# Gate and up weights of an expert in rows of 16 KB and one transfer, in place of two arrays with rows of 8 KB

## The chip, the cores and the metric

One NeuronCore of a Trainium2 chip runs the whole program. The metric is the device time of one execution in microseconds (us), the median of several. The engines are TensorE (PE), VectorE (DVE), ScalarE (ACT), GpSimd (POOL) and SyncE (SP), which issues most transfers; 16 DMA engines move the data of all queues.

## What is computed

One layer of a decoder trunk for 1024 prompt tokens and 64 sample tokens, in float32: a projection, a convolution branch and a windowed attention branch, their merge, and a mixture of 32 experts with the top 2 of one group. The change touches the experts only:

```python
xb = xn[tok_buf].reshape(n_blocks, MOE_BLOCK, D_MODEL)       # MOE_BLOCK = 128, D_MODEL = 1024
def expert_block(args):
    xblk, e = args
    hid = jax.nn.silu(xblk @ w_gate[e]) * (xblk @ w_up[e])    # D_EXPERT = 256
    return hid @ w_down[e]
yb = lax.map(expert_block, (xb, blk_expert)).reshape(rows, D_MODEL)
return jnp.zeros_like(xn).at[tok_buf].add(yb * w_buf[:, None])
```

There are 1088 tokens and 2 experts for each, 2176 pairs, spread over at least 32 blocks of 128 slots.

## The kernel before

The phases run one behind the other. Norm, attention, sample, convolution and merge take the time up to 1163 us and have no part in the change. The last one, `ffn_phase`, first goes through 9 tiles of 128 tokens (output projection, norm, routing), then through the expert blocks.

**Data.** Matrix products have the precision of float32 by splitting each operand into a high and a low half in float16 and doing three products (`mm3`, lines 69 to 71). So each block's weights are loaded as float32 and then cut: ACT writes the high half, DVE the low half (float32 minus high). The gate and up weights of an expert are 8 chunks of 128 rows by 512 columns. The host lays them out by partition: 8 x 512 float32 numbers, 16 KB, for each of the 128 partitions. `layout` puts chunks 0 to 3 in `w_gu0` and chunks 4 to 7 in `w_gu1`, each with 8 KB a partition. `w_dn` has 8 KB a partition.

**Buffers.** There are four float32 buffers for `w_gu` and four for `w_dn` (`gu32`, `d32`; two of each in own tiles `e_gu`, `e_d`, one each inside `xnT` and `big`), and two of the cut halves (`gu`, `d`), one for even and one for odd blocks. Block b uses buffer b mod 2 for the first two, then (b - 2) mod 4.

**Loads (SP).** `load_expert` (lines 1569 to 1576) issues loads 0 to 7 at fixed places, `load_any` (lines 1612 to 1619) the rest in a loop of 6 rounds of four, blocks 8 to 31. Before it overwrites a buffer, SP waits until DVE has finished with the half in question: `gu_low[0]` and `gu_low[1]` count DVE's subtractions of half 0 and half 1, `d_low` those of `w_dn`. SP issues in order: half 0, half 1, `w_dn`.

**Gathers and scatters (POOL).** Tokens of a block are gathered from `hn_dram` by an indirect DMA (line 1656), and the weighted results added into `y_all` by another (line 1667), 4 KB a row. A block's pairs fill its slots from partition 0 upwards; slots without a pair are out of bounds and move nothing. Both have two buffers, so a gather or scatter has to be over two blocks later. Ahead of the loop the pairs themselves are scattered to DRAM (line 1643) and loaded back by SP.

**A block in the loop.** ACT's `body(b)`: gate, cut of half 0 of block b + 2 (line 1734), result of block b - 1 (line 1761, waits for the scatter of b - 3), rows of block b + 2 (1744), hidden (1754), cut of half 1 of block b + 2 (1734), cut of `w_dn` of block b + 1 (1740). DVE's `body(b)`: gate (1968, 1971), low half of half 0 (1951), rows (1962), hidden (1975), low half of half 1 (1951), low half of `w_dn` (1957). PE: gate-up of block b, down of b - 1, turn of b + 2 (2089), turn of the hidden rows (2107).

Of the kernel before, what the change touches and what calls it, by code (L numbers as in the profile page):

```python
# [20 lines left out]
ds = bass.ds  # L21
# [3 lines left out]
KC = D // P  # L25
# [1387 lines left out]
def ffn_phase(nc, sem, g, A):  # L1413


    with ExitStack() as c:
# [103 lines left out]
                                    "scat", "ctl"))  # L1520
        pairs_ld, late_ld, xg_zero, all_out = sem("e_pairs_ld"), sem("e_late_ld"), sem("e_xg_zero"), sem("e_all_out")
        gather_go, scatter_go = sem("e_gather_go"), sem("e_scatter_go")
        gu_ld = tuple((sem("e_gu_ld0" + n), sem("e_gu_ld1" + n)) for n in "abcd")
        d_ld = tuple(sem("e_d_ld" + n) for n in "abcd")
        xg_ld = (sem("e_xg_ld0"), sem("e_xg_ld1"))
        y_st = (sem("e_y_st0"), sem("e_y_st1"))
# [29 lines left out]
        @block.sync  # L1556
        def _(sp):
            def load_x(t):
                if t > 2:
                    sp.wait_ge(h_st, 16 * (t - 2))  # L1560
                    sp.wait_ge(hn_done, t - 2)
                sp.dma_start(x_in[:, t % 3], A["x_all"][t * P:(t + 1) * P, :]).then_inc(x_ld[t % 3], 16)

            def store_h(t):
                sp.wait_ge(h_done, t + 1)
                sp.dma_start(A["y_all"][t * P:(t + 1) * P, :], x_in[:, t % 3]).then_inc(h_st, 16)

            def load_expert(b, f, used):
                for half in range(2):
                    if used:  # L1570
                        sp.wait_ge(gu_low[half], used)
                    sp.dma_start(gu32[f][:, halves[half]], A[("w_gu0", "w_gu1")[half]][b].rearrange("p (k n) -> p k n", k=HK)
                                 ).then_inc(gu_ld[f][half], 16)
                if used:
                    sp.wait_ge(d_low, used)
                sp.dma_start(d32[f], A["w_dn"][b].rearrange("p (k n) -> p k n", k=2)).then_inc(d_ld[f], 16)

            load_x(0)
            sp.dma_start(r32, A["w_rt"]).then_inc(r_ld, 16)
            sp.dma_start(gain[:], rows_on_partitions(A["norm_ffn_g"], P, D)).then_inc(gain_ld, 16)  # L1580
            load_x(1)
            sp.dma_start(rb[:], rows_on_partitions(A["b_rt"], P, RP)).then_inc(rb_ld, 16)
            load_x(2)
            sp.dma_start(iota[:], A["c_iota"]).then_inc(iota_ld, 16)
            sp.dma_start(upper[:], A["c_upper"]).then_inc(upper_ld, 16)
            sp.dma_start(A["pair_dram"].rearrange("(p n) a -> p (n a)", p=P), A["c_unused"]).then_inc(unused_st, 16)
            load_expert(0, 0, 0)
            load_expert(1, 1, 0)
            for t in range(TT):
                store_h(t)  # L1590
                if t + 3 < TT:
                    load_x(t + 3)
                if t == 4:
                    load_expert(2, 0, 1)
                if t == 6:
                    load_expert(3, 1, 2)
            sp.wait_ge(mm, TT)
            load_expert(4, 2, 0)
            load_expert(5, 3, 0)
            by_column = A["pair_dram"].rearrange("(p n) a -> n p a", p=P)  # L1600
            sp.dma_start(pairs[:, NE:].rearrange("p b a -> p (b a)"), A["c_unused"][:, 0:4 * NOV]).then_inc(late_ld, 16)
            sp.wait_ge(scat, 16 * 2 * TT)
            sp.dma_start(pairs[:, 0:NE], A["pair_dram"].rearrange("(p n) a -> p n a", p=P)[:, 0:NE]).then_inc(pairs_ld, 16)
            load_expert(6, 0, 3)
            load_expert(7, 1, 4)
            few = rounds(sp)
            sp.wait_ge(late_ld, 16)
            for i in range(NOV):
                col = sp.value_load(ctl[0:1, NBLK + i:NBLK + i + 1], min_val=0, max_val=NCOL - 1)  # L1609
                sp.dma_start(pairs[:, NE + 2 * i + 1], by_column[ds(col, 1)].rearrange("n p a -> (n p) a")).then_inc(late_ld, 16)  # L1610

            def load_any(b, f):
                e = sp.value_load(ctl[0:1, ds(b, 1)], min_val=0, max_val=NE - 1)
                for half in range(2):
                    sp.wait_ge(gu_low[half], b - 3)
                    sp.dma_start(gu32[f][:, halves[half]].rearrange("p k n -> p (k n)"),
                                 A[("w_gu0", "w_gu1")[half]][ds(e, 1)].rearrange("a p n -> (a p) n")).then_inc(gu_ld[f][half], 16)
                sp.wait_ge(d_low, b - 3)
                sp.dma_start(d32[f].rearrange("p k n -> p (k n)"),
                             A["w_dn"][ds(e, 1)].rearrange("a p n -> (a p) n")).then_inc(d_ld[f], 16)  # L1620

            with sp.Fori(0, few) as v:
                for q in range(4):
                    load_any(4 * v + 8 + q, (q + 2) % 4)
# [86 lines left out]
        def _(act):  # L1711
# [18 lines left out]

            def cut(load, p, half):
                f, need = load
                act.wait_ge(gu_ld[f][half], need)
                act.activation(gu_h[:, p, halves[half]], gu32[f][:, halves[half]], ACT.Copy,  # L1734
                               scale=S_W).then_inc(gu_high[half], 1)

# [501 lines left out]
def layout(x_prompt, x_sample, state_conv, cache_k, cache_v, norm_attn_g, w_in, q_norm_g, k_norm_g, rel_bias,  # L2238
           attn_sinks, w_dw, b_dw, conv_ln_g, conv_ln_b, w_conv_out, b_conv_out, w_attn_out, w_out, norm_ffn_g,
           w_grp, b_grp, w_router, b_router, w_gate, w_up, w_down):  # L2240

    f = np.float32
    x_all = np.zeros((TP, D), f)
    x_all[0:SEQ] = x_prompt.reshape(SEQ, D)
    x_all[SEQ:T] = x_sample.reshape(TS, D)

    def chunks(w):

        return w.reshape(KC, P, -1, P).transpose(2, 1, 0, 3).reshape(-1, P, KC * P)

    def by_channel(v):
        return v.reshape(KC, P).T


    gated = np.stack([chunks(w_in[:, COL_GB:COL_GB + D]), chunks(w_attn_out)], 1).reshape(2 * KC, P, KC * P)
    bag = np.stack([chunks(w_in[:, c:c + D]) for c in (COL_B, COL_A, COL_GA)] + [gated[0:KC]], 1)
    def in_turn(w):

        return w.reshape(NG, EPG, P, -1).transpose(1, 0, 2, 3).reshape(NE, P, -1)

    gu = in_turn(np.concatenate([w_gate, w_up], 2).reshape(NE, KC, P, 2 * DE).transpose(0, 2, 1, 3))
    dn = in_turn(w_down.reshape(NE, 2, P, D).transpose(0, 2, 1, 3))

    dist = 2 * P - 1 - np.arange(RW)
    n = np.maximum(dist, 0)
    large = NB // 2 + (np.log(np.maximum(n, 1).astype(f) / f(NB // 2)) / f(np.log(128 / (NB // 2)))
                       * f(NB - NB // 2)).astype(np.int32)
    bucket = np.where(n < NB // 2, n, np.minimum(large, NB - 1))
    inside = (dist >= 0) & (dist < WIN)
    c_bucket = ((bucket[None, :] == np.arange(NB)[:, None]) & inside[None, :]).astype(f)  # L2270
    c_mask = np.broadcast_to(np.where(inside, f(0), f(NEG)), (NH, RW))
    return {k: np.ascontiguousarray(v) for k, v in {
        "x_all": x_all, "norm_attn_g": norm_attn_g, "w_in": w_in, "gq2": np.concatenate([q_norm_g] * 2)[:, None],
        "k_norm_g": k_norm_g, "rel_bias": rel_bias, "attn_sinks": attn_sinks,
        "cache_k": cache_k.reshape(NSEQ, WIN, KVW), "cache_v": cache_v.reshape(NSEQ, WIN, KVW),
        "ckT": cache_k.transpose(3, 2, 0, 1).reshape(HD, NKV * NSEQ, WIN),
        "cvT": cache_v.transpose(1, 0, 2, 3).reshape(WIN, NSEQ, KVW),
        "stateT": state_conv.transpose(2, 0, 1), "tapsT": w_dw.T.reshape(KC, P, TAPS).transpose(1, 0, 2),
        "conv_vecs": np.stack([by_channel(b_dw), by_channel(conv_ln_g), by_channel(conv_ln_b)], 1),
        "b_conv_outT": by_channel(b_conv_out),  # L2280
        "w_feat": np.concatenate([bag.reshape(-1, P, KC * P), gated[KC:], chunks(w_conv_out)]),
        "w_out": w_out, "norm_ffn_g": norm_ffn_g,
        "w_rt": np.concatenate([w_grp, np.zeros((D, 8 - NG), f), w_router], 1).reshape(KC, P, RP).transpose(1, 0, 2),
        "b_rt": np.concatenate([b_grp, np.full(8 - NG, NEG, f), b_router]), "w_gu0": gu[:, :, 0:gu.shape[2] // 2], "w_gu1": gu[:, :, gu.shape[2] // 2:], "w_dn": dn,
        "c_ident": np.eye(P, dtype=f), "c_bucket": c_bucket, "c_mask": c_mask,
        "c_iota": np.broadcast_to(np.arange(NE, dtype=f), (P, NE)),
        "c_upper": np.triu(np.ones((P, P), f), 1), "c_unused": unused_slots()}.items()}
# [23 lines left out]
```

## Time and profile before

| | us |
|---|---|
| median of 3 runs (1677.76 to 1679.7) | 1678.14 |
| the profiled execution | 1678.61 |
| its span, first to last instruction | 1677.0 |
| expert blocks, from the first gather to the end | 376.0 |

| engine | busy us | share of the span |
|---|---|---|
| PE | 1335.1 | 80% |
| DVE | 1147.2 | 68% |
| ACT | 637.7 | 38% |
| POOL | 249.1 | 15% |

The hardware queue q1 carries SP's transfers, 32416 packets and 156.99 MB; the software queue q0 carries POOL's, 16144 packets and 36.84 MB. A busy share of DMA is the mean over the 16 engines: a share of 0.68 can be all engines busy two thirds of the time, or two thirds of them busy all the time. Shares over an average of the whole span hide stages; the expert blocks have the last 376 us.

### The profile page before, as it was taken

To read this page: it belongs to the slowest core of one execution; us is meant where nothing else is said; L and a number is where in the kernel's file an instruction comes from. 1 tells how busy PE (TensorE), PEld (TensorE's weight loads), DVE (VectorE), ACT (ScalarE), POOL (GpSimd) and SP (SyncE) were. 2 spreads that over 40 slices of the span, in tenths; PEclk is the share of its full clock that TensorE was granted. 3 is DMA by queue.
4 is the path that set the end of the run, shared out by engine and by line. 5 is a ranking of instruction groups with operands and counts; after the bars stand their busy time and mean duration, and the time that the engine had idled before them with its cause. 6 is when DMAs were issued, how large, how long until landed. Compare 5 with 4: busy or idle time off the path is not lost. (4 is left out here: it accounts for less than half of the span.)

```text
span 1677.0 us, 25763 instructions
## 1 busy us (share of the span) xinstructions
PE 1335.1 (80%) x8692; PEld 805.5 (48%) x8692; DVE 1147.2 (68%) x1550; ACT 637.7 (38%) x916; POOL 249.1 (15%) x259
## 2 busy tenths in 40 slices
PE   2668877877159989989798797888995779888885
PEld 2245655555135656556465454454553444434442
DVE  5356666666414999999999856453556578777773
ACT  5234444444312101111011236332411568676673
POOL 0110000000400000000000000000114345333321
PEclk9988899899559999989899799999997889999998
DMA  6510000000303132221122100643666469999972
GB/s 236 133 27 1 0 0 0 0 3 3 63 20 115 35 81 59 70 71 52 57 58 67 65 13 28 216 147 118 261 240 239 130 237 371 334 332 323 337 267 48
DMA packets 50926, 203.53 MB, mean 121 GB/s; under 512 B 14272, under 2 KB 15424, under 8 KB 38272
## 3 DMA queue, kind: packets, MB, share of 16 engines
q1 hardware_dynamic: 32416, 156.99, 26.2%
q0 software_dynamic: 16144, 36.84, 8.5%
q10 hardware_dynamic: 2304, 8.95, 2.0%
q8 instruction: 31, 0.51, 0.1%
q14 instruction: 31, 0.25, 0.1%
HBM read 180.92 MB, written 39.72 MB: 132 GB/s over the span
## 5 line engine op out<-in xcount | busy, mean ns | idle before, releaser
L1104 DVE SCALAR_TENSOR_TENSOR big<-c_region,c_taps,big 128x1024 f32 x240 | 308.1, 1284 | 0.0
L69 PE MATMUL c_psb<-xnT,f_w_h 128*128 128x364 f16 x456 | 146.1, 320 | 17.1 <-DVE f_w_l L1072 17.1
L70 PE MATMUL c_psb<-xnT,f_w_h 128*128 128x364 f16 x456 | 146.0, 320 | 0.0
L71 PE MATMUL c_psb<-xnT,f_w_l 128*128 128x364 f16 x456 | 145.9, 320 | 0.0
L69 PE MATMUL c_psa<-xnT,f_w_h 128*128 128x364 f16 x312 | 102.9, 330 | 23.7 <-DVE c_gate_b L1078 23.7
L70 PE MATMUL c_psa<-xnT,f_w_h 128*128 128x364 f16 x312 | 102.6, 329 | 0.0
L71 PE MATMUL c_psa<-xnT,f_w_l 128*128 128x364 f16 x312 | 102.5, 328 | 0.0
L69 PE MATMUL o_psH<-e_gu,big 128*128 128x512 f16 x256 | 98.8, 386 | 1.4 <-issue 1.3
L1951 DVE SCALAR_TENSOR_TENSOR e_gu<-e_gu 128x2048 f16<-128x2048 f32 x36 | 82.4, 2290 | 25.4 <-ACT e_gu L1734 25.4
L71 PE MATMUL o_psH<-e_gu,big 128*128 128x512 f16 x256 | 98.8, 386 | 0.0
L70 PE MATMUL o_psH<-e_gu,big 128*128 128x512 f16 x256 | 98.7, 385 | 0.0
L69 PE MATMUL a_psP<-big,xnT 128*128 128x512 f16 x216 | 83.8, 388 | 2.1 <-ACT qkv L340 1.4
L70 PE MATMUL a_psP<-w_qkv_l,xnT 128*128 128x512 f16 x216 | 83.4, 386 | 0.0
L71 PE MATMUL a_psP<-big,xnT 128*128 128x512 f16 x216 | 83.1, 385 | 0.0
L1734 ACT ACTIVATE e_gu<-e_gu 128x2048 f16<-128x2048 f32 x36 | 68.6, 1909 | 33.4 <-DMA e_gu<-w_gu 33.3
L1667 POOL DMA_INDIRECT y_all<-o_hn,e_idx_y x32 | 66.9, 2090 | 94.2 <-ACT o_hn L1761 67.7
L446 DVE SCALAR_TENSOR_TENSOR a_pT_l<-a_psT,a_pT_h 128x1024 f16<-128x1024 f32 (+1 forms) x32 | 37.0, 1158 | 60.2 <-ACT a_pT_h L384 60.2
L69 PE MATMUL c_psa<-oT_h,f_w_h 128*128 128x364 f16 x192 | 62.4, 325 | 18.9 <-DVE c_gate_b L1078 18.9
L330 POOL TENSOR_TENSOR a_rs<-a_ms,neg_half 128x20 f32<-128x20 f32 x9 | 31.8, 3538 | 301.4 <-DVE a_ms L427 301.4
L69 PE MATMUL m_ps<-caT,f_w_h 128*128 x192 | 62.2, 324 | 17.1 <-ACT m_conv L1337 9.1
L368 ACT ACTIVATE big<-big,a_ntop 128x256 f32<-128x256 f32 (+1 forms) x128 | 61.5, 483 | 29.9 <-DVE a_ntop L472 29.8
L972 ACT ACTIVATE f_w_h<-f_w 128x1024 f16 (+1 forms) x42 | 43.4, 1052 | 71.6 <-PE c_psa L71 46.8
(341 smaller groups left out, 3450.0 us busy)
## 6 DMA issues: line engine op xcount, KB each, us to landing
e_gu<-w_gu SPq DMA_DIRECT2D x36, 1024.0 KB, 32.7
f_w<-w_feat SPq DMA_DIRECT2D x48, 512.0 KB, 3.7
e_d<-w_dn SPq DMA_DIRECT2D x18, 1024.0 KB, 30.2
xnT<-w_gu SPq DMA_DIRECT2D x14, 1024.0 KB, 33.0
big<-w_gu SPq DMA_DIRECT2D x14, 1024.0 KB, 33.1
m_gates<-gates POOLq DMA_DIRECT2D x8, 1092.0 KB, 5.8
xnT<-w_dn SPq DMA_DIRECT2D x7, 1024.0 KB, 30.2
big<-w_dn SPq DMA_DIRECT2D x7, 1024.0 KB, 29.9
```

The costliest lines, as they stand in the source:

```text
L69: pe.matmul(out, stat[0], mov[0], start=start, stop=False)
L70: pe.matmul(out, stat[0], mov[1], start=False, stop=False)
L71: return pe.matmul(out, stat[1], mov[0], start=False, stop=stop)
L330: pool.tensor_tensor(rs[:], ms[:], g.neg_half[:, 0:NH + NKV], ALU.pow).then_inc(rs_done, 1)
L368: act.activation(prob[:, s, r, lo:], prob[:, s, r, lo:], ACT.Exp, bias=ntop[:, s, r:r + 1], accum_out=den[:, s, r:r + 1]).then_inc(exp_don ...
L446: dve.scalar_tensor_tensor(dst, psT[:, 0:dst.shape[1]], S_X, high, op0=ALU.mult, op1=ALU.subtract).then_inc(T_free, 1)
L972: act.activation(w_h[:, pos], slot32(n).rearrange("p (k m) -> p k m", k=KC), ACT.Copy, scale=S_W).then_inc(w_high, 1)
L1104: dve.scalar_tensor_tensor(y_p, glu[:, p, j:j + SEQ], tap, y_p, op0=ALU.mult, op1=ALU.add).then_inc(tap_done, 1)
L1667: pool.indirect_dma_start(out=A["y_all"], out_offset=bass.IndirectOffsetOnAxis(ap=idx_y[:, p:p + 1], axis=0), in_=y_o[:, p], in_offset=Non ...
L1734: act.activation(gu_h[:, p, halves[half]], gu32[f][:, halves[half]], ACT.Copy, scale=S_W).then_inc(gu_high[half], 1)
L1951: dve.scalar_tensor_tensor(gu_l[:, p, halves[half]], gu32[load[0]][:, halves[half]], S_W, gu_h[:, p, halves[half]], op0=ALU.mult, op1=ALU. ...
```

## The change

The host keeps the gate and up weights as one array `w_gu`, 16 KB a partition. `load_expert` and `load_any` issue one transfer of 2 MB for it, after the waits for both halves' subtractions. Each buffer has one semaphore in place of two, and both of ACT's cuts wait for it. What is computed, the cuts, the subtractions and the order of work on PE, DVE, ACT and POOL stay.

```diff
-        gu_ld = tuple((sem("e_gu_ld0" + n), sem("e_gu_ld1" + n)) for n in "abcd")
+        gu_ld = tuple(sem("e_gu_ld" + n) for n in "abcd")
...
             def load_expert(b, f, used):
-                for half in range(2):
-                    if used:
-                        sp.wait_ge(gu_low[half], used)
-                    sp.dma_start(gu32[f][:, halves[half]], A[("w_gu0", "w_gu1")[half]][b].rearrange("p (k n) -> p k n", k=HK)
-                                 ).then_inc(gu_ld[f][half], 16)
+                if used:
+                    sp.wait_ge(gu_low[0], used)
+                    sp.wait_ge(gu_low[1], used)
+                sp.dma_start(gu32[f], A["w_gu"][b].rearrange("p (k n) -> p k n", k=KC)).then_inc(gu_ld[f], 16)
...
             def load_any(b, f):
                 e = sp.value_load(ctl[0:1, ds(b, 1)], min_val=0, max_val=NE - 1)
-                for half in range(2):
-                    sp.wait_ge(gu_low[half], b - 3)
-                    sp.dma_start(gu32[f][:, halves[half]].rearrange("p k n -> p (k n)"),
-                                 A[("w_gu0", "w_gu1")[half]][ds(e, 1)].rearrange("a p n -> (a p) n")).then_inc(gu_ld[f][half], 16)
+                sp.wait_ge(gu_low[0], b - 3)
+                sp.wait_ge(gu_low[1], b - 3)
+                sp.dma_start(gu32[f].rearrange("p k n -> p (k n)"),
+                             A["w_gu"][ds(e, 1)].rearrange("a p n -> (a p) n")).then_inc(gu_ld[f], 16)
...
             def cut(load, p, half):
                 f, need = load
-                act.wait_ge(gu_ld[f][half], need)
+                act.wait_ge(gu_ld[f], need)
...
-        "w_gu0": gu[:, :, 0:gu.shape[2] // 2], "w_gu1": gu[:, :, gu.shape[2] // 2:], "w_dn": dn,
+        "w_gu": gu, "w_dn": dn,
```

One block's load in SP's loop, before (`TENSOR_LOAD` and `ISA` fetch the expert's number, the sizes are partitions x float32 numbers):

```order
L1613 TENSOR_LOAD r_ctl
L1613 ISA x2
L1615 REGISTER_ALU
L1616 ISA
L1616 DMA big<-w_gu 128x2048 x2
L1619 DMA big<-w_dn 128x2048
```

And now:

```order
L1612 TENSOR_LOAD r_ctl
L1612 ISA x2
L1613 REGISTER_ALU
L1615 ISA
L1615 DMA big<-w_gu 128x4096
L1618 ISA
L1618 DMA big<-w_dn 128x2048
```

Two issues of 2048 numbers a partition have become one of 4096, and the address of `w_dn` is worked out by an instruction of its own.

## Rows read from the trace of the kernel before

**Rows 1.** Page, part 6, DMA issues: count, KB each, median us to landing.
```profile
e_gu<-w_gu SPq DMA_DIRECT2D x36, 1024.0 KB, 32.7
...
e_d<-w_dn SPq DMA_DIRECT2D x18, 1024.0 KB, 30.2
```

**Rows 2.** Chain that ended last, loop: start us, us, what.
```profile
1423.69 36.87 DMA e_gu<-w_gu
1460.57 1.92 ACT e_gu L1734
...
1464.72 2.30 DVE e_d L1957
1468.65 37.06 DMA e_gu<-w_gu
```

**Rows 3.** Windows: busy us by engine (instructions), PE clock, DMA share, GB/s.
```profile
1424.00:1636.00 212.00, 176.34 (x866) 86.88 (x865) 167.22 (x131) 149.75 (x131) 73.58 (x74) 0.98 0.89 318
...
1476.00:1480.00 4.00, 2.15 (x15) 1.49 (x14) 3.64 (x4) 1.90 (x3) 1.27 (x2) 1.00 0.68 219
1480.00:1486.00 6.00, 6.00 (x30) 2.75 (x29) 4.61 (x4) 5.43 (x6) 2.14 (x3) 1.00 1.00 369
```

**Rows 4.** Timeline of SP: start us, us, issue.
```profile
1395.17 0.33 SPq L1619 DMA_DIRECT2D e_d<-w_dn  x1
...
1480.42 2.11 SPq L1616 DMA_DIRECT2D xnT<-w_gu  x2
```

**Rows 5.** DMA queues from 1460 to 1640: packets, MB, share of 16 engines.
```profile
q1 hardware_dynamic: 6477, 47.12, 67.1%
q0 software_dynamic: 4456, 9.03, 20.0%
```

**Rows 6.** DMA queues from 1368 to 1376, weights with almost nothing beside them.
```profile
q1 hardware_dynamic: 427, 3.15, 95.5%
```

**Rows 7.** Windows, 1174 to 1180, loads 0 and 1.
```profile
1174.00:1180.00 6.00, 6.00 (x29) 2.72 (x28) 2.48 (x3) 1.15 (x2) 0.57 (x1) 1.00 1.01 426
```

**Rows 8.** DMA queues from 1005 to 1050, stores of gates, 4368 B a row.
```profile
q10 hardware_dynamic: 432, 1.68, 9.2%
```

**Rows 9.** Page, part 3, the queue that fetches instructions.
```profile
q8 instruction: 31, 0.51, 0.1%
```

**Rows 10.** Timeline of ACT: start us, us, instruction, idle time ahead and its releaser.
```profile
1386.52 1.11 ACT L1761 ACTIVATE o_hn<-o_psH,big 128x1024 f32<-128x1024 f32 x1 [12.95 <-DMA y_all<-o_hn,e_idx_y]
...
1627.26 1.91 ACT L1734 ACTIVATE e_gu<-e_gu 128x2048 f16<-128x2048 f32 x1 [3.21 <-DMA e_gu<-w_gu]
...
1631.30 1.91 ACT L1734 ACTIVATE e_gu<-e_gu 128x2048 f16<-128x2048 f32 x1
...
1641.23 1.91 ACT L1734 ACTIVATE e_gu<-e_gu 128x2048 f16<-128x2048 f32 x1 [0.86 <-DMA e_gu<-w_gu]
```

**Rows 11.** Timeline of DVE behind the last load.
```profile
1643.17 2.29 DVE L1951 SCALAR_TENSOR_TENSOR e_gu<-e_gu 128x2048 f16<-128x2048 f32 x1 [0.98 <-ACT e_gu L1734]
...
1647.58 0.41 DVE L1968 SCALAR_TENSOR_TENSOR xnT<-xnT,o_psH 128x256 f32<-128x256 f32 x1
```

**Rows 12.** DMA queues from 1282 to 1285, load 5 beside a store of POOL.
```profile
q1 hardware_dynamic: 104, 0.81, 65.1%
q0 software_dynamic: 105, 0.43, 34.5%
```

**Rows 13.** Gathers (L1656), 1430 to 1636, issue to landing.
```profile
DMA to landing us min/median/max: 8.2/8.5/9.8
```

**Rows 14.** Scatter-adds (L1667), 1430 to 1636, issue to landing.
```profile
DMA to landing us min/median/max: 10.2/10.8/12.0
```

**Rows 15.** Waits of SP: releaser, us in total, times, longest us.
```profile
SPq L1619 <- DVE e_d L1957: 179.4, 21, 20.9
...
SPq L1616 <- DVE e_gu L1951: 0.2, 1, 0.2
```

**Rows 16.** Timeline of POOL, first scatter of the last pairs.
```profile
1292.14 0.96 POOL L1643 DMA_INDIRECT pair_dram<-r_pair,r_dest  x1 [6.45 <-DVE r_dest L1916]
```

More of the change, by code:

```diff
@@ L2283, in layout @@
         "w_rt": np.concatenate([w_grp, np.zeros((D, 8 - NG), f), w_router], 1).reshape(KC, P, RP).transpose(1, 0, 2),
-        "b_rt": np.concatenate([b_grp, np.full(8 - NG, NEG, f), b_router]), "w_gu0": gu[:, :, 0:gu.shape[2] // 2], "w_gu1": gu[:, :, gu.shape[2] // 2:], "w_dn": dn,
+        "b_rt": np.concatenate([b_grp, np.full(8 - NG, NEG, f), b_router]), "w_gu": gu, "w_dn": dn,
         "c_ident": np.eye(P, dtype=f), "c_bucket": c_bucket, "c_mask": c_mask,
```

## The prediction

> **What bounds the kernel now.** I read the page for the stages first: the loads of `w_gu` and `w_dn` are 32 of each, 64 and 32 issues over three target tiles, and they land after 30 us and more [rows 1]; nearly all belong to the last 370 us, the expert stage. Only there can the edit act. Then the chain of that stage: in its second half it is a ring of one DMA piece of 37 us, one ACT cut (L1734), DVE's subtractions, and the next DMA piece [rows 2]. One turn of four blocks takes 1468.65 - 1423.69 = 45.0 us, 11.3 us for a block. Then the queues. The stage looks bound by DMA, yet the mean busy share is 0.89, and just ahead of a new issue it falls to 0.68, returning to 1.00 right behind it [rows 3, 4], while loads issued long before are still landing after more than 30 us [rows 1]. So some of the 16 engines run dry while the rest have three blocks queued. The reason I read from the code: a block has 128 slots but 2176 pairs over 32 blocks fill 68 of them on average, always from partition 0 upwards, so gathers and scatter-adds fall almost wholly on the lower 64 partitions, while weights fall on all. The Trainium skill, "DMA: Bandwidth & Descriptors", The descriptor swizzle, has eight engines writing partitions 0 to 63 and eight the rest; the trace names no engine, but a share that drops towards one half fits.
>
> The work of such a late engine in one block: 24 weight rows of 8 KB and about 15 packets of 4 KB (60 gathered and 60 scattered rows over 8 engines). A 4 KB packet of the software queue costs 0.200 x 180 x 16 us over 9.03 MB / 4096 B = 261 ns, and a weight row 336 ns on average in the loop [rows 5], but 318 ns with nothing beside it: 0.955 x 8 x 16 us over 384.5 rows [rows 6], or 311 ns from 426 GB/s at share 1.01 [rows 7]. 24 x 0.311 + 15 x 0.261 = 11.4 us, the period. The late half of the engines bounds the stage, not latency and not the compute engines.
>
> **Term 1, fewer packets.** One row of 16 KB replaces two of 8 KB. What a packet costs beyond its bytes: the gates' stores, 4368 B a row, take 0.092 x 45 x 16 us over 384.6 rows = 172 ns [rows 8]; against 318 ns at 8192 B that leaves 5 ns when drawn down to zero bytes, against 311 ns it leaves 14 ns. I take the middle, 10 ns. Loads 8 to 31 meet a loaded queue: 24 x 8 rows per engine x 10 ns = 1.9 us less (1.0 to 2.7). No row of the trace shows a 16 KB load into a tile. The nearest above is the instruction queue, 31 packets in 0.51 MB and 0.1% of the span [rows 9], 0.43 to 1.3 us each; that queue fetches code and moves little, so I keep it as the far upper end and not as the value. The lower end, besides the fixed cost, is that the 25 ns by which a row costs more in the loop than alone (336 - 311) are per packet too: then 24 x 8 x 25 ns = 4.8 us more are saved.
>
> **Term 2, the later cut.** The cut of half 0 waited for the first megabyte, now it waits for both. Where a load lands late, cut 1 started as its half landed; now cut 0 starts then, and result, rows, hidden stand between it and cut 1. From cut 0 to an unwaited cut 1 is 1631.30 - 1627.26 = 4.0 us [rows 10]. Within the loop this is covered twice. From the landing DVE needs 4.0 + 1.9 for the cut + 2.3 + 2.3 for the two subtractions [rows 2, 11] = 10.5 us, still under 11.3. And the refill leaves 4 us later, but its queue on the late engines is some 30 us deep. The cover is gone at the end. The last load's second half lands at 1641.23 [rows 10]; behind it stand DVE's subtraction at 1643.17 and, right behind the one of `w_dn`, the gate at 1647.58 [rows 11], on which the last turn and the last gate-up hang. So plus 4.0 us if it lands where it did (0 to 4.0).
>
> **Term 3, who is served first.** From 1282 to 1285 both queues have work and 104 packets of one and 105 of the other go through, though one has 8 KB and the other 4 KB [rows 12]. So engines alternate packet by packet. A 16 KB packet doubles what a load gets per turn, and gathers and scatters give way. Per block they needed 15 x (0.261 + 0.311) = 8.6 us of 11.3; with weights averaging (8 x 0.62 + 8 x 0.31) / 16 = 0.465 us a packet they need 15 x 0.726 = 10.9 us. That is nearly always. Gathers and scatters that landed after 8.5 and 10.8 us [rows 13, 14] will take at least 11 and 14, and loads get ahead of them. They have room: a scatter's buffer is wanted again two bodies later, 22.6 us. The late engines' total work is unchanged, but when the last load lands, about one block's gather and scatter remain to be served: 15 x 0.261 = 3.9 us earlier (0 to 3.9). The Trainium skill, "DMA: Bandwidth & Descriptors", Queues, rings and completion order, also has round-robin by packet, but a packet there is typically 9 to 17 descriptors. By that rule one load's 8 rows on an engine would be one turn in both kernels, this term would be 0, and the sum would be +2.1; the equal counts above speak for one row a turn.
>
> **What costs nothing.** The merged issue waits for `gu_low[0]` and `gu_low[1]`. SP already sat at the wait for `d_low` for 179.4 us in 21 cases, and at the wait for the first half's buffer only once, 0.2 us [rows 15]; when it passes `d_low` both halves of the next block are free. Queued behind the added wait is only the next `w_dn`. One issue less a block on SP is hidden by the same wait. Ahead of the loop no cut of `w_gu` waited for a load. At 1292.14 POOL waits 6.45 us for DVE with the pair scatter [rows 16]; the six scatters ahead of it, with two packets each on an engine (pairs, and the count at the end), lose 12 x 0.155 = 1.9 us beside loads 4 and 5, hidden by that wait, and would cost one for one beyond it. At 1386.52 ACT has waited 12.95 us for a scatter [rows 10]; its 18 packets or so with weights at 0.465 us cost 18 x 0.155 = 2.8 us more. This is on the chain, but the late engines are busy with loads 8 to 11 (30 us of work) and the next load leaves SP at 1395.17 [rows 4], so only compute slack is spent. If that queue ran dry, 2.8 us would be added.
>
> **Sum.** -1.9 + 4.0 - 3.9 = -1.8 us. On the profile's span of 1677.0 that is 1675.2. The profiled execution took 1678.61, 0.5 above the median 1678.14; on the median I predict **1676.3 us**.
>
> **Rivals.**
> *The tail pays in full, slower.* Loads don't get ahead (term 3 near 0) and the fixed cost is small or the rows go as two packets of 8 KB, so that the change doesn't do what it says: 4.0 - 0 to 1.0 = +3.0 to +4.0, up to 1682.1. The place is the last body; it decides once terms 1 and 3 together are under 0.6 us. The equal packet counts speak against it, the lack of a 16 KB load for it. Chance 0.16. The Trainium skill, "Perfetto Trace Analysis", DMA Optimizations, says that smaller pieces let work start sooner; that is term 2, and the row bears it out only for the last body.
> *Larger packets carry more, faster.* The 25 ns of contention are per packet: 1676.3 - 4.8 = 1671.5. For it speaks 336 against 311; against it, that the late engines' sum already meets 11.3 us with 311. Chance 0.20. The Trainium skill, "Perfetto Trace Analysis", DMA Optimizations, also says that larger transfers saturate the memory better; it speaks of steps up to 8 KB.
> *The order of service stays, same.* If an engine takes all 8 rows that it has of a load in one turn, a turn has the same bytes before and now; term 3 is 0 and the rest stays: -1.9 + 4.0 = +2.1, 1680.2. It decides if turns go by transfer and not by row; the equal counts [rows 12] speak against it, though only in one window. Chance 0.10.
> *Forecast*, the terms offset within 3 us: 0.54.
>
> **Numbers.** About 0.2% (3.4 us) is what a measurement can tell from no change. Range: from the faster rival, 1671.5, to just over the full tail, 1682.5. Same 0.54 + 0.10 = 0.64, faster 0.20, slower 0.16.
>
> **What would show it.** Term 1: the hardware queue has some 4600 packets fewer (4096 rows, and 512 that count a transfer's end), and weights' time per MB falls by some 1 to 3%. Term 3: scatters land at 14 us or more, gathers above 10; loads (now 2 MB) in well under 33 us; ACT's idle time moves from L1734 waiting for `w_gu` to L1761 waiting for `y_all`. Term 2: 4 us between the last cut 0 and cut 1, with the last load landing near 1636 instead of 1641. Wrong if the packet count stays, if the period leaves 11.3 us by more than 0.2, or if scatters grow past 22.6 us: then ACT's result stands still with weights landed while the DMA share falls. The late engines' full load of 11.4 us speaks against such idle time.

## The result: slower by 0.3 to 0.4%

The changed kernel took **1685.46 us** (median of 9 runs, 1681.6 to 1688.95), the kernel before beside it 1678.14 us (1677.21 to 1680.57). The ratio is 1.0040, 95% interval 1.0027 to 1.0052. The prediction of 1676.3 us (1671.5 to 1682.5) missed it, on the wrong side. Repeated (`a0_changed_again`) it was 1.0027 (1.0013 to 1.0042), a little under the 0.3 to 0.5% expected for it. Both intervals lie above 1.

> The changed kernel once more, beside the others on one chip, as their reference. All theories: 0.3 to 0.5% over the kernel before, and scatter-adds that land after about 20 us.

### The profile page after: what moved, and what is told of

The parts are those of the page before. It is cut to its first block and busy times, and to the rows that moved or that the text cites. A ratio compares the mean times of both kernels' runs of the same rounds, so it can differ in the third digit from the quotient of the medians.

```text
span 1683.8 us, 25759 instructions
## 1 busy us (share of the span) xinstructions
PE 1346.5 (80%) x8692; PEld 808.7 (48%) x8692; DVE 1147.5 (68%) x1550; ACT 636.3 (38%) x916; POOL 276.2 (16%) x259
## 3 DMA queue, kind: packets, MB, share of 16 engines
q1 hardware_dynamic: 27808, 156.98, 26.2%
## 5 line engine op out<-in xcount | busy, mean ns | idle before, releaser
L69 PE MATMUL o_psH<-e_gu,big 128*128 128x512 f16 x256 | 103.0, 402 | 1.6 <-issue 1.5
L71 PE MATMUL o_psH<-e_gu,big 128*128 128x512 f16 x256 | 102.7, 401 | 0.0
L70 PE MATMUL o_psH<-e_gu,big 128*128 128x512 f16 x256 | 102.5, 400 | 0.0
L1961 DVE SCALAR_TENSOR_TENSOR big<-o_psT,big 128x1024 f16<-128x1024 f32 x32 | 39.1, 1223 | 58.1 <-ACT big L1743 58.0
L1760 ACT ACTIVATE o_hn<-o_psH,big 128x1024 f32<-128x1024 f32 x32 | 35.7, 1115 | 93.9 <-DMA y_all<-o_hn,e_idx_y 81.3
## 6 DMA issues: line engine op xcount, KB each, us to landing
e_gu<-w_gu SPq DMA_DIRECT2D x18, 2048.0 KB, 22.9
```

The lines of the kernel that those rows point to most:

```text
L69: pe.matmul(out, stat[0], mov[0], start=start, stop=False)
L70: pe.matmul(out, stat[0], mov[1], start=False, stop=False)
L71: return pe.matmul(out, stat[1], mov[0], start=False, stop=stop)
L1760: act.activation(y_o[:, p], psY, ACT.Copy, scale=weight(b)).then_inc(y_out, 1)
L1961: dve.scalar_tensor_tensor(xT_l[:, p], psT[:], S_X, xT_h[:, p], op0=ALU.mult, op1=ALU.subtract).then_inc(xT_low, 1)
```

## The profile after

Line numbers from 1575 on are smaller by one than before: ACT's cut is L1733, its result L1760, POOL's gather L1655, its scatter L1666. The profiled execution took 1685.46 us with a span of 1683.8.

Page, part 3, the hardware queue (packets, MB, share), and part 6, what a load takes to land (compare [rows 1]):

```profile
q1 hardware_dynamic: 27808, 156.98, 26.2%
...
e_gu<-w_gu SPq DMA_DIRECT2D x18, 2048.0 KB, 22.9
```

A load of 2 MB now lands after 22.9 us, where 1 MB took 32.7. The hardware queue has 32416 - 27808 = 4608 packets fewer, exactly 4096 rows and 512 packets that mark a transfer's end (32 transfers fewer, 16 of them each): the rows go as single packets of 16 KB.

Queues from 1460 to 1640, the stretch of [rows 5] (packets, MB, share of 16 engines):

```profile
q1 hardware_dynamic: 4334, 46.83, 66.7%
q0 software_dynamic: 4593, 9.29, 20.8%
```

0.667 x 180 x 16 us over 46.83 MB is 41.0 us for a MB, and before it was 0.671 x 2880 / 47.12 = 41.0 too. The packets' records of that kind give a median of 611 ns for a 16 KB row and 309 ns for an 8 KB row: 7 ns are saved for each pair of rows, and the total doesn't show it.

Landing of the scatters (min/median/max, us; 1430 to 1640), where [rows 14] has 10.8:

```profile
DMA to landing us min/median/max: 6.3/20.4/20.9
```

Twice as long. Waits from 1366 to 1640 (who waited for whom: us in total, times, longest):

```profile
ACT o_hn L1760 <- DMA y_all<-o_hn,e_idx_y: 81.3, 23, 9.3
...
POOL e_idx_y L1662 <- DMA y_all<-o_hn,e_idx_y: 33.7, 16, 7.5
...
ACT e_gu L1733 <- DMA xnT<-w_gu: 4.2, 1, 4.2
```

Before, ACT's large wait was that of a cut for its weights (`ACT e_gu L1734 <- DMA e_gu<-w_gu`, 32.4 us in 14 cases, and with the buffers in `big` and `xnT` 63.0 us in 27). Now only one cut in the stage waits for weights, 4.2 us, and 23 of the 32 results wait for a scatter. The chain that ended last has changed its members with it (start us, us, what):

```profile
1388.16 20.12 DMA y_all<-o_hn,e_idx_y
...
1428.26 0.89 PE o_psT L2088 x8
...
1429.98 0.77 POOL xnT L1655
...
1433.31 19.73 DMA y_all<-o_hn,e_idx_y
...
1523.14 20.33 DMA y_all<-o_hn,e_idx_y
1543.66 1.12 ACT o_hn L1760
...
1545.67 20.42 DMA y_all<-o_hn,e_idx_y
...
1591.14 20.37 DMA y_all<-o_hn,e_idx_y
1611.66 1.12 ACT o_hn L1760
```

[rows 2] had loads of 37 us there. Now scatters are 52.7% of the chain from 1380 on, and no load is in it. One ring is that of scatter and result. A result buffer is written at 1543.66, its scatter is under way from 1545.67 and lands 20.42 us later, and the result two blocks on, which wants the same buffer, starts at 1566.25. So 22.6 us for two blocks, 11.3 us for a block. That is the period that the loads had set before. The chain isn't this ring all the time: from 1408.75 to 1432.55 it runs over ACT, DVE, PE's turn of the gathered rows and POOL's next gather, behind which POOL issues the scatter. Once over both ways takes 45.2 us for four blocks (scatters from 1388.16 and from 1433.31), 11.3 us for a block again. The stage's period hardly moved; what sets it did.

Then where do 7 us come from? From the blocks that never ran at 11.3 us. ACT's results in the timeline (start us, us, instruction, idle time ahead and its releaser), **before** the change, behind the one at 1386.52 of [rows 10]:

```profile
1404.34 1.12 ACT L1761 ACTIVATE o_hn<-o_psH,big 128x1024 f32<-128x1024 f32 x1 [0.52 <-PE o_psH L71]
...
1413.29 1.11 ACT L1761 ACTIVATE o_hn<-o_psH,big 128x1024 f32<-128x1024 f32 x1 [0.60 <-PE o_psH L71]
...
1422.69 1.12 ACT L1761 ACTIVATE o_hn<-o_psH,big 128x1024 f32<-128x1024 f32 x1 [0.54 <-PE o_psH L71]
```

and **after** it:

```profile
1386.16 1.11 ACT L1760 ACTIVATE o_hn<-o_psH,big 128x1024 f32<-128x1024 f32 x1 [9.32 <-DMA y_all<-o_hn,e_idx_y]
...
1408.47 1.11 ACT L1760 ACTIVATE o_hn<-o_psH,big 128x1024 f32<-128x1024 f32 x1 [3.21 <-DMA y_all<-o_hn,e_idx_y]
...
1419.55 1.11 ACT L1760 ACTIVATE o_hn<-o_psH,big 128x1024 f32<-128x1024 f32 x1 [3.10 <-DMA y_all<-o_hn,e_idx_y]
...
1430.83 1.11 ACT L1760 ACTIVATE o_hn<-o_psH,big 128x1024 f32<-128x1024 f32 x1 [2.86 <-DMA y_all<-o_hn,e_idx_y]
```

In both kernels no cut of these four blocks waits for weights. Before, the blocks took 9.0 us each, the pace of PE and its partners; after, 11.1 to 11.3, each with some 3 us of waiting for a scatter. From 1386 on, four blocks bring the new kernel from 0.36 us ahead to 8.14 us behind. The new kernel makes up part of it in the long loop: from the 11th to the 28th result the period was (1629.08 - 1434.38) / 17 = 11.45 us before and (1634.48 - 1441.95) / 17 = 11.33 after, 2.2 us in all. The loads did end earlier (the last packet at 1636.7 in place of 1643.3), but nothing was waiting for them. At the 31st result the kernel is 5.26 us behind, and the last interval is 6.53 us in place of 4.84. The last matmuls took 0.63 us each in place of 0.38: the granted clock was 0.76 from 1662 to 1668, having fallen to the lower of its two levels, 1.2 GHz, at 1665.16. PE had stood idle for 1.96 us until 1664.28, but it did so before the change as well (until 1659.01), and there the clock stayed at 1.00 from 1655 to 1662. Windows (PE clock, DMA share and GB/s at the end of the row), after:

```profile
1424.00:1636.00 212.00, 181.69 (x873) 89.16 (x872) 169.21 (x131) 148.90 (x131) 96.57 (x72) 0.96 0.89 320
...
1640.00:1684.00 44.00, 24.53 (x103) 10.72 (x101) 16.76 (x16) 14.81 (x16) 13.04 (x8) 0.79 0.21 32
```

The DMA share of the loop is the 0.89 of [rows 3]. The mean granted clock of the loop fell from 0.98 to 0.96.

## Experiments

The measure is the ratio to the kernel before, run on the same chip; the intervals are at 95%. The kernel before itself had medians of 1678.14, 1680.86, 1681.3 and 1679.42 us in the four groups of runs.

| kernel | median us | ratio (interval) | scatters land after, us | results 1 to 31, us |
|---|---|---|---|---|
| before | | 1 | 10.8 | 329.9 |
| changed | 1685.46 | 1.0040 (1.0027 to 1.0052) | 20.4 | 334.6 |
| changed, again | 1686.41 | 1.0027 (1.0013 to 1.0042) | 20.4 | 338.2 |
| `e1` 8 KB rows, later cut | 1683.39 | 1.0015 (1.0003 to 1.0027) | 10.7 | 332.6 |
| `e4` one array alone | 1682.37 | 1.0004 (0.9991 to 1.0017) | 10.8 | 331.1 |
| `e5` 4 KB rows | 1683.68 | 1.0018 (1.0004 to 1.0033) | 10.2 | 336.7 |
| `e2` changed, 4 result buffers | 1677.07 | 0.9977 (0.9963 to 0.9991) | 25.1 | 325.4 |
| `e3` before, 4 result buffers | 1680.17 | 0.9994 (0.9980 to 1.0007) | 10.8 | 330.2 |
| `e11` changed, down in 4 KB rows | 1680.45 | 1.0013 (1.0000 to 1.0026) | 12.6 | 331.8 |
| `e6` before, pairs spread | 1643.90 | 0.9782 (0.9763 to 0.9802) | 10.4 | 294.7 |
| `e7` changed, pairs spread | 1653.15 | 0.9823 (0.9803 to 0.9843) | 16.0 | 302.0 |
| `e10` `e1`, pairs spread | 1649.02 | 0.9816 (0.9802 to 0.9831) | 9.9 | 297.6 |
| `e8` changed, spread, 4 buffers | 1643.86 | 0.9799 (0.9783 to 0.9816) | 19.9 | 296.1 |
| `e9` before, spread, 4 buffers | 1646.90 | 0.9804 (0.9788 to 0.9819) | 10.1 | 294.8 |

The last two columns are of one profiled execution each, landings from 1430 to 1600. The last column is the time from ACT's first result to its 31st. The changed kernel stands there twice with 334.6 and 338.2, so differences of some 3 us in the last column mean nothing. The kernels with the spread, `e6` to `e10`, have 5 runs each, the others 9 to 12. The theories and rivals with a letter are those of the expectations.

**The later cut alone.** The changed kernel's waits and its one semaphore, but two transfers of 8 KB rows:

```diff
-                sp.dma_start(gu32[f], A["w_gu"][b]...).then_inc(gu_ld[f], 16)
+                for half in range(2):
+                    sp.dma_start(gu32[f][:, halves[half]], A["w_gu"][b][:, half * 2048:half * 2048 + 2048]...).then_inc(gu_ld[f], 16)
...
-                act.wait_ge(gu_ld[f], need)
+                act.wait_ge(gu_ld[f], 2 * need)
```

> The changed kernel's waits with packets of 8 KB: one array, but each block's gate and up weights come in two transfers of 1 MB with rows of 8 KB, issued after the waits for both subtractions, with one semaphore that both cuts wait for. Theory S (a packet of 16 KB takes double time per turn, so scatter-adds starve): scatter-adds land after about 11 us as before, ACT waits for loads again, and only the later cut of the last block remains, 1678 to 1682 us. Rival W (the later cut and the joint wait are the cost): no better than the changed kernel, 1685 us.

1.0015 is 2.5 us (0.5 to 4.5 by the interval): the later cut has a price of its own, and scatters land as before (10.7 us). With 1683.39 us it came out above theory S's 1678 to 1682, and its interval overlaps that of the changed kernel's repeat; the landings and waits tell the two apart. The cuts wait for their weights again (waits of `e1`, 1366 to 1600):

```profile
ACT e_gu L1737 <- DMA e_gu<-w_gu: 28.1, 9, 5.2
ACT e_gu L1737 <- DMA big<-w_gu: 18.7, 4, 5.1
ACT e_gu L1737 <- DMA xnT<-w_gu: 15.0, 5, 4.8
```

**Four result buffers.** The results go to four buffers in turn in place of two, with four semaphores, so that a result waits for the scatter of four blocks before. This needs that no block beyond the 32 is in use, which holds for these inputs. With the changed kernel (`e2`) and with the one before (`e3`):

```diff
-        y_o = hn
+        y_o = [hn[:, 0], hn[:, 1], x_in[:, 0], x_in[:, 1]]
-        y_st = (sem("e_y_st0"), sem("e_y_st1"))
+        y_st = tuple(sem("e_y_st%d" % i) for i in range(4))
```

> The changed kernel (16 KB rows) with four result buffers, indices and semaphores for the scatter-adds in place of two, so that a result waits for the scatter of four blocks earlier. Theory S with two buffers as the ring that binds: scatter-adds still land after 20 us or more, but ACT hardly waits for them, blocks 8 to 12 run at 9 us again, and the time falls by 5 to 9 us to 1676 to 1681 us. Rival W: no change, 1685 us.

> Control: the kernel before (8 KB rows) with the same four result buffers. Theory S: its scatter-adds land in 11 us and bind only once at block 8 (12.95 us of waiting, most of it for the pair columns), so it gains 0 to 4 us, 1674 to 1678 us, less than the same edit gains with 16 KB rows. If four buffers gain as much here as there, the result buffers were no matter of the packet size.

With 16 KB rows two more buffers are worth 1685.46 to 1677.07 us or, by ratios, 0.5 to 0.6%; with 8 KB rows 0.06%, nothing that can be told (1680.17 us, above the 1674 to 1678 expected, beside a kernel before at 1680.86). So two more result buffers take the price of the change away. No result waits for a scatter any more in `e2`; the next in line are the gathers, which land after 20.2 us there and have two buffers too (waits of `e2`, 1366 to 1640):

```profile
POOL e_idx L1650 <- DMA xnT<-hn_dram,e_idx: 97.6, 21, 5.7
PE o_psT L2087 <- DMA xnT<-hn_dram,e_idx: 42.1, 24, 6.4
```

Where the time comes back is to be read from ACT's results in the timelines (us behind the first result, one profiled execution each):

| kernel | 7th | 10th | 28th | 31st |
|---|---|---|---|---|
| before | 68.0 | 95.5 | 301.9 | 329.9 |
| changed | 69.5 | 103.1 | 306.7 | 334.6 |
| `e2` changed, 4 result buffers | 62.0 | 93.7 | 296.4 | 325.4 |
| `e3` before, 4 result buffers | 64.6 | 93.7 | 302.5 | 330.2 |
| `e1` 8 KB rows, later cut | 67.1 | 99.2 | 304.3 | 332.6 |

Most of what `e2` gains on the changed kernel, 7.5 of 9.2 us, is there at the 7th result: behind the load of the pairs the 6th no longer waits 9.32 us for a scatter. From the 7th to the 10th it takes 31.7 us, the changed kernel 33.5 and the one before 27.5. So the expectation that these blocks would run at 9 us again missed: without the waits for scatters, gathers hold them up.

**One array, nothing else.** `w_gu` with 16 KB a partition, read by two transfers of 8 KB pieces with the waits of before:

```diff
-                    sp.dma_start(gu32[f][:, halves[half]], A[("w_gu0", "w_gu1")[half]][b]...)
+                    sp.dma_start(gu32[f][:, halves[half]], A["w_gu"][b][:, half * 2048:half * 2048 + 2048]...)
```

> The layout alone: one array with 16 KB a partition, but two transfers with rows of 8 KB, two semaphores and all waits as in the kernel before. Theory S and rival W: as before, 1678 us within 2. If the pitch of 16 KB between rows of 8 KB costs or gains, it shows here alone.

1.0004 (0.9991 to 1.0017): no price of the layout in memory can be told; scatters land after 10.8 us.

**Smaller rows.** The same array in four transfers of 4 KB pieces:

> The dose in the other direction: one array, waits and semaphores of the kernel before, but four transfers of 512 KB with rows of 4 KB for each block's gate and up weights. Theory S: a weight packet takes half the time per turn, so scatter-adds land sooner than 10.8 us (8 to 10), results never wait for them in the loop, and loads land later. Packets are 16 more per block on an engine: at 5 to 14 ns each 2 to 5 us over 24 blocks, 1680 to 1684 us if the kernel before is at 1679. Rival P (what a packet costs is all that rows change, and 16 KB should then have gained): the same, so the landing times decide.

Scatters landed after 10.2 us, where 8 to 10 was expected, and gathers after 8.6: with 8 KB rows it was 10.8 and 8.5. Landings hardly changed, and the kernel was slower by 0.18%; the DMA share from 1420 to 1630 rose from 0.90 to 0.95 for the same GB/s. Row size and landing are not proportional downwards. Why not stays open.

**More load packets beside 16 KB rows.** Is it the size of the packet, or how many there are? The changed kernel, with `w_dn` in two transfers of 4 KB rows:

```diff
-                sp.dma_start(d32[f], A["w_dn"][b]...).then_inc(d_ld[f], 16)
+                for k in range(2):
+                    sp.dma_start(d32[f][:, k], A["w_dn"][b][:, k * D:k * D + D]).then_inc(d_ld[f], 16)
...
-                act.wait_ge(d_ld[f], need)
+                act.wait_ge(d_ld[f], 2 * need)
```

> The changed kernel, but the down weights of an expert come in two transfers of 4 KB rows in place of one of 8 KB rows. On the late engines a block then brings 8 packets of 16 KB and 16 of 4 KB, 24 load packets to 15 rows of gathers and scatters as before the change, where the changed kernel has 16 packets to 15. Theory A (a row of the gathers and scatters gets one turn for each load packet; with 16 load packets to 15 rows their queue never empties, which is why scatters land after 20.4 us): the queue empties again, scatters land after 11 to 14 us, results stop waiting for them, and the time falls to 1678 to 1682 us. Theory B (it is the single packet of 16 KB that keeps a row waiting, whatever comes between): scatters land after 17 us or more, and the time stays within 3 us of the changed kernel's, 1683 to 1689 us.

Landing of the scatters of `e11`:

```profile
DMA to landing us min/median/max: 11.4/12.6/13.4
```

Its waits from 1366 to 1640:

```profile
ACT e_gu L1735 <- DMA e_gu<-w_gu: 34.2, 10, 5.0
...
ACT o_hn L1762 <- DMA y_all<-o_hn,e_idx_y: 8.9, 1, 8.9
```

The 16 KB rows are all still there, and scatters land after 12.6 us in place of 20.4; results wait for one once in place of 23 times, and the time is 1680.45, within theory A's 1678 to 1682. Theory B, which wanted 17 us or more, falls. The time alone would not show it: 1.0013 (1.0000 to 1.0026) overlaps the repeat of the changed kernel, 1.0027 (1.0013 to 1.0042). On a late engine a block brings 24 load packets before, 16 after, 24 in `e11`, against 15 packets of gathers and scatters. The software queue shows the same in the records of its 4 KB packets: of the 200 slices of 1 us from 1430 to 1630, those in which at most two of them started are 33 before, **none** after, 15 in `e11`. With one turn each, 16 load packets a block would leave no time in which the other queue is empty. This is argued, with two limits. `e11` has smaller load packets as well as more of them: their mean in the records is 310 ns ((8 x 611 + 16 x 159) / 24 from the medians), about the 309 of before the change, so number and mean size are not told apart. And with the spread (below) the slices don't go with the landings: `e7` and `e8` have 14 and 16 of them, and their scatters land after 16.0 and 19.9 us. What is left of the price (1.0013) is about that of the later cut (1.0015).

**The engines' halves.** The prediction rested on gathers and scatters falling on half of the engines. Slots 0 to 63 on the even partitions and 64 to 127 on the odd ones:

```diff
-            sp.dma_start(pairs[:, 0:NE], A["pair_dram"]...[:, 0:NE]).then_inc(pairs_ld, 16)
+            for h in range(2):
+                sp.dma_start(pairs[h::2, 0:NE], A["pair_dram"]...[64 * h:64 * h + 64, 0:NE]).then_inc(pairs_ld, 16)
...
-            pool.wait_ge(pairs_ld, 16)
+            pool.wait_ge(pairs_ld, 32)
```

> The kernel before, but the pairs of the first 32 blocks are read with ranks 0 to 63 on even and 64 to 127 on odd partitions, so that a block of 68 pairs lies on all 128 partitions and not on the lower 64. Two loads in place of one. If half of the engines bound the loop, their work falls from 11.4 to 24 x 0.311 + 8.5 x 0.261 = 9.7 us a block, close to the 9.0 us of compute: 1.6 us less in some 19 blocks, 1645 to 1655 us. If the DMA as a whole or latency bound it, no change.

> The changed kernel with the same spread. Theory S: gathers and scatter-adds need 8.5 x (0.261 + 0.465) = 6.2 us of an engine's 9.7 us, no longer nearly all, so scatter-adds land in under 15 us and 16 KB rows cost nothing against 8 KB rows: within 3 us of the kernel before with the spread. Rival W: 5 us or more slower than that one, as without the spread.

Before with the spread is 2.2% faster than before, 37 us, a little more than the 1645 to 1655 us expected. Windows of `e6`:

```profile
1430.00:1590.00 160.00, 148.96 (x755) 75.54 (x754) 146.76 (x116) 132.00 (x117) 96.20 (x67) 1.00 1.02 389
```

From 1430 to 1590 the DMA share is 1.02 with 389 GB/s, against 0.92 and 332 without the spread. Latency isn't what the spread saves: scatters land after 10.4 us in place of 10.8, gathers after 9.1 in place of 8.5. The half-idle engines were real, and they were the bound. No trace names an engine, so this rests on the share, the rate and the time. With 16 KB rows the gain is less by 9 us (1653.15 against 1643.9), and the same wait is there, although an engine now has some 8 packets of gathers and scatters a block instead of 15. Landing of its scatters, and its wait from 1366 to 1600:

```profile
DMA to landing us min/median/max: 10.5/16.0/18.0
```

```profile
ACT o_hn L1762 <- DMA y_all<-o_hn,e_idx_y: 45.1, 21, 9.1
```

Theory S had landings under 15 us and a time within 3 us of `e6`; both missed. So the count of turns above is no full account: with half of the rows on an engine, scatters of the kernel before still land after 10.4 us, and those of the changed kernel after 16.0.

**Spread, taken apart.** Four result buffers on top of `e7` and of `e6`, and the later cut with 8 KB rows:

> Rows of 16 KB, pairs spread over the even and odd partitions, four result buffers. With 16 KB rows and the spread alone the last stage took 1653.15 us, 9.25 us more than with 8 KB rows and the spread (1643.9), and its results waited 45.1 us for scatters that landed after 16.0 us instead of 10.4 us. Theory L (the long landing of scatters in the way of the results is the whole price of 16 KB rows): with four buffers nothing waits for a scatter, and the time falls to 1641 to 1646 us. Theory O (16 KB rows cost the other transfers something that no buffer gives back, the gathers' landing above all, 14.8 us against 9.1 us): 1648 to 1653 us, with PE or the column copies waiting for gathers.

> Rows of 8 KB, the spread, four result buffers. Theory L: scatters land after 10 to 11 us, two buffers are wanted again after two periods of 9.6 us = 19 us, so two more gain nothing but the one wait of 10.6 us at the first of the late blocks, at most 4 us of it on the path: 1641 to 1645 us. Theory O expects the same. If it comes below 1640 us, scatters hold up more than the trace shows.

> The spread, two transfers of 8 KB rows, but the waits of the changed kernel: both halves are asked for when both buffers are free, and the first cut waits for both to land. It tells the later cut from the row size where the loads are no longer slowed by half of the engines. Theory L (row size): scatters land after 10 to 11 us and the time is that of 8 KB rows with the spread plus what the later cut cost without it (1683.39 less 1680.86 = 2.5 us): 1644 to 1648 us. Theory C (the later cut is what costs 9 us with the spread): 1651 to 1655 us.

`e8` at 1643.86 is within theory L's 1641 to 1646: with four buffers 16 KB rows cost nothing beside 8 KB rows, 0.9799 against 0.9804. Its gathers still land after 16.8 us, and POOL waits 40.1 us for them, but 1643.86 us is no more than `e9` takes. `e9`, expected at 1641 to 1645, came to 1646.90 and is no better than `e6`. The fall of the sum from 9 us is less clean than L had it: `e10` came to 1649.02, a little above L's 1644 to 1648 and under C's 1651 to 1655, and by ratios (0.9816 against 0.9823 of `e7`) the later cut could be most of it. By the profiles the results' stretch gives the later cut 297.6 - 294.7 = 2.9 us and the rows 302.0 - 297.6 = 4.4 us, no more than the scatter of two profiles of one kernel. How the 9 us are shared with the spread stays open.

The fastest are `e6`, `e8` and `e9`, level within their intervals, 2.0 to 2.2% faster than the kernel before. The simplest of them, the kernel before with the pairs spread, is the edit shown above and nothing else.

## Why the prediction was wrong

**The bound** was right: half of the engines ended last, 11.3 us a block. `e6`, the direct test, gave 37 us.

The Trainium skill, "DMA: Bandwidth & Descriptors", The descriptor swizzle, was what led there from a share of 0.68, and the gain by the spread agrees with its eight engines for the lower partitions.

**Term 1**, fewer packets, -1.9 us. The mechanism is there, 4608 packets fewer and 7 ns saved a pair of rows in place of the 10 assumed: 24 x 8 x 7 ns = 1.3 us by the same sum. The time per MB that was to fall by 1 to 3% stayed at 41.0 us. By the packets' means from 1430 to 1640 the reason is that `w_dn` gave it back: a 16 KB row took 636 ns where two of 8 KB took 2 x 335, but a `w_dn` row 364 in place of 335.

**Term 2**, the later cut, +4.0 us. Right in sign, and as a price of its own 2.5 us (`e1`, 0.5 to 4.5 by the interval). Its place was another in the one profile of `e1`: the prediction had the loop covered and the price in the last body. `e1` lost 4.6 us on the kernel before from the 7th to the 10th result, with waits of 0.90 and 3.43 us for weights that before did not wait, and from the 28th to the last result it took 33.1 us in place of 32.8. Nor is it so that "ahead of the loop no cut of `w_gu` waited for a load": the one at 1371.66 had waited 1.53 us, and it waits 4.22 us after the change, hidden by the scatter's wait behind it. In the changed kernel itself nothing waited there: the last cuts, at 1640.53 and 1644.70, found their weights.

**Term 3**, who is served first, -3.9 us. The order was right: loads ended 6.6 us earlier, scatters and gathers gave way. By four buffers one can estimate what terms 1 and 3 would have brought. `e2` against `e3` is 0.9977 - 0.9994 = -0.0017, 2.9 us; less the 2.5 us of the later cut, -5.4 us, where the two terms said -5.8. The intervals together leave some 4 us to either side of this.

**The step that failed** stands in term 3, where it puts the longer landings at no cost: "They have room: a scatter's buffer is wanted again two bodies later, 22.6 us." It rests on landings of "at least 11 and 14 us". The working had the number that speaks against this: gathers and scatters would need 10.9 of 11.3 us. Scatters landed after 20.4 us, not 14, and gathers after 19.5 (`a0_changed_again`), not 11. The likely reason is that a queue that is busy for 97% of the time has no pause in which it catches up, so that scatter and gather wait behind each other. With ACT's 1.1 us and POOL's issue that makes 22.5 us for two blocks, and the room was used up to the last microsecond. The prediction named nearly this as what would prove it wrong ("if scatters grow past 22.6 us"), without the 2.1 us for result and issue, and gave it neither a rival nor a chance. ACT's idle time moving to the result, 81.3 us of it, stood there as a sign that term 3 was right.

**The second half of the same step** is that the room was measured against the loop's mean of 11.3 us. Ahead of it four blocks ran at 9.0 us, with a need of 2 x 9.0 = 18.0 us. There a landing of 20.4 us with its 2.1 costs 4.5 us for two blocks, 9.0 for four, and 8.5 us were lost by 1430.83. `e2` shows that the scatters are not alone in this: without a wait for them the last three of these blocks still took 31.7 us in place of 27.5. The gathers' room was short there as well, and two more result buffers gain their time mainly at the wait ahead of these blocks. The prediction had looked at just this place (at 1386.52, "only compute slack is spent") and looked at one wait, not at the four blocks behind it. The same thing is why the end moved out although the loads ended earlier: the sum took the end as the last load's landing and a fixed tail, and the tail now hung on scatters.

**Rivals.** *Larger packets carry more* (0.20) didn't occur. *The order of service stays* (0.10) is out by the packet records below. Its working has a slip: if an engine took all 8 rows of a transfer in one turn, the turn would have grown from 8 rows of 8 KB to 8 rows of 16 KB, so the longer landings alone don't rule it out. *The tail pays in full* (0.16) had the sign, up to 1682.1, but by another mechanism: its price of 3 to 4 us is the later cut alone in the last body, and `e1` shows 2.5 us, elsewhere.

How long a turn is, `e1` and `e11` can't tell, for the number of transfers changes in them along with that of rows. The packet records can. From 1430 to 1590 I take each 4 KB row of the software queue that starts within 4 ns of the end of exactly one other packet: before, 1037 of 1082 follow a load's row and 40 a row of their own queue; after, 1030 of 1112 and 71. So a turn is one row here. The Trainium skill, "DMA: Bandwidth & Descriptors", Queues, rings and completion order, has turns of typically 9 to 17 descriptors. The trace doesn't agree with it.

Shown by runs: two more result buffers take the price away, and only with 16 KB rows (`e2`, `e3`); the long landing comes from the 16 KB rows and not from the array (`e4`) or the waits (`e1`), and more and smaller load packets shorten it (`e11`). The later cut has up to 2.5 us or so of the price. Only argued: how the rest is shared between scatters and gathers in the blocks at 9.0 us, that the queue's emptiness, not some other effect of the packets' number or size, is what shortens the landing, and what the lower clock at the end (1.7 us in this profile) has to do with it; the repeat, `e4`, `e10` and `e11` have the same 6.53 us there, `e1` to `e3` and `e5` to `e9` have 4.85 or less, so it doesn't go with the size of the rows.

## What to carry to other kernels

Where two queues share the DMA engines, larger packets in one can be taken from the other, as here (landings of 20.4 us in place of 10.8): ask for each transfer of the smaller queue how long it may take before its buffer is wanted, and hold that against the fastest stretch of the loop, not against its mean. Such a sum of turns is not enough: here 97% of the period went with landings of 20.4 us, and 64% (6.2 of 9.7 us, `e7`) still with 16.0. Before making the loads of a DMA-bound stage cheaper, see whether all 16 engines carry the same; here spreading the pairs over the partitions gave 37 us, where terms 1 and 3 together said 5.8.

## What was not expected of the hardware

- A packet of 16 KB takes 611 ns where two of 8 KB take 618: going from 8 to 16 KB gained almost nothing, while scatters beside it took 20.4 us in place of 10.8.
- Rows of 4 KB did not shorten the landings (10.2 us), nor did half as many rows on an engine (10.4 us). So most of these 10 us don't follow the loads' rows, and no run here says what they are made of.
- Two profiled executions of the changed kernel differ by 7.1 us in span (1683.8 and 1690.9) at mean clocks of 0.904 and 0.898, and the medians of the kernel before lay 3 us apart in two of its groups of runs (1678.14 and 1681.3). Effects of 0.1 to 0.2%, such as that of `e1`, stand just clear of this with 12 runs.
